# Layer norm tails of a two-block network: the normalization moved to ScalarE, the first turn moved between the last products

## The reference, cut to what matters

```python
def layer_norm(x, g, b):
    mu = x.mean(-1, keepdims=True)
    var = jnp.square(x - mu).mean(-1, keepdims=True)
    y = (x - mu) * lax.rsqrt(var + LN_EPS)
    return y * g + b

for l in range(2):
    mix = hybrid_mixer(x, ...)                      # ends in  y @ w_out[l]
    x = layer_norm(ALPHA * x + mix, ln1_g[l], ln1_b[l])
    ffn = conv_glu_ffn(x, ...)                      # ends in  hidden @ w_down[l]
    x = layer_norm(ALPHA * x + ffn, ln2_g[l], ln2_b[l])
```

## Time and profile before

| | |
|---|---|
| Median of 3 runs | 3353.11 us (3350.36 to 3353.71) |
| Profiled execution | 3352.97 us |
| Span in its profile | 3351.2 us |
| Mean granted clock of TensorE | 0.936 of full speed |
| Busy: TensorE, VectorE, ScalarE, GpSimd | 3006.5, 2480.5, 1366.8, 457.8 us |

### The profile page before, as it was taken

One profiled execution on the slowest core, in us unless ns is written; L12 is line 12 of the kernel. 1 busy time (PEld: TensorE's weight loads), 2 busy tenths in 40 slices (PEclk: granted clock), 3 DMA queues, 4 the chain that ended last, 5 costly groups with the idle time before them and its releaser, 6 DMA issues. The chain is left out here.

```text
span 3351.2 us, 40382 instructions
## 1 busy us (share of the span) xinstructions
PE 3006.5 (90%) x13932; PEld 2421.2 (72%) x13932; DVE 2480.5 (74%) x2722; ACT 1366.8 (41%) x1618; POOL 457.8 (14%) x252
## 2 busy tenths in 40 slices
PE   6997899989878999969997999995997979999995
PEld 5776778867666888747775888884774767888884
DVE  3556798564566997575867999996476658999996
ACT  1131111001231111045235777774336326777774
POOL 0110122321101113210000000001423000000001
PEclk8998899989988999979997999997998979999997
DMA  4231565223233663246219999994212339999993
GB/s 156 69 158 63 178 225 176 101 87 100 97 137 96 207 226 116 86 124 156 75 58 333 373 370 373 385 389 153 101 50 84 120 119 366 375 383 385 385 387 141
DMA packets 346507, 667.25 MB, mean 199 GB/s; under 512 B 21936, under 2 KB 138604, under 8 KB 338172
## 3 DMA queue, kind: packets, MB, share of 16 engines
q1 hardware_dynamic: 339612, 642.58, 54.6%
q0 software_dynamic: 6752, 22.81, 2.0%
HBM read 612.20 MB, written 53.13 MB: 199 GB/s over the span
## 5 line engine op out<-in xcount | busy, mean ns | idle before, releaser
L2683 DVE TENSOR_TENSOR expert_w_low<-expert_w_raw,expert_w_high 128x2048 fp32r<-128x2048 f32 x290 | 663.1, 2289 | 65.4 <-ACT expert_w_high L2644 65.3
L2644 ACT CAST expert_w_high<-expert_w_raw 128x2048 fp32r<-128x2048 f32 x290 | 554.9, 1914 | 181.6 <-PE bank L144 178.7
L142 PE MATMUL bank<-expert_w_high,expert_x_high 128*128 128x512 f32 x928 | 379.7, 409 | 5.2 <-DVE expert_w_low L2683 4.3
L142 PE MATMUL bank<-first_XH,first_w_high 128*128 128x512 f32 x912 | 365.9, 401 | 12.3 <-DVE first_w_low L221 12.3
L144 PE MATMUL bank<-expert_w_high,expert_x_low 128*128 128x512 f32 x928 | 365.3, 394 | 0.0
L143 PE MATMUL bank<-expert_w_low,expert_x_high 128*128 128x512 f32 x928 | 364.0, 392 | 0.0
L143 PE MATMUL bank<-first_XL,first_w_high 128*128 128x512 f32 x912 | 358.5, 393 | 0.0
L144 PE MATMUL bank<-first_XH,first_w_low 128*128 128x512 f32 x912 | 358.3, 393 | 0.0
L221 DVE TENSOR_TENSOR first_w_low<-first_w_raw,first_w_high 128x2048 fp32r<-128x2048 f32 (+2 forms) x104 | 305.3, 2935 | 3.6
L219 DVE CAST first_w_high<-first_w_raw 128x2048 fp32r<-128x2048 f32 (+2 forms) x104 | 120.2, 1156 | 185.2 <-PE bank L144 174.3
L2516 POOL DMA_INDIRECT expert_x_rows<-h_rows,slot_token x58 | 66.4, 1144 | 1265.4 <-PE bank L2549 862.8
(11 more groups left out here) (523 smaller groups left out, 6007.6 us busy)
## 6 DMA issues: line engine op xcount, KB each, us to landing
expert_w_raw<-in_moe_w_gate_dram SPq DMA_DIRECT2D x116, 1024.0 KB, 8.3
expert_w_raw<-in_moe_w_up_dram SPq DMA_DIRECT2D x116, 1024.0 KB, 13.4
expert_w_raw<-in_moe_w_down_dram SPq DMA_DIRECT2D x58, 1024.0 KB, 13.7
modulation<-in_moe_w_down_dram SPq DMA_DIRECT2D x58, 1024.0 KB, 13.8
ffn_mod_w<-in_ada_w_dram SPq DMA_DIRECT2D x48, 1024.0 KB, 5.0
first_w_raw<-in_w_up_dram SPq DMA_DIRECT2D x88, 512.0 KB, 6.2
first_w_raw<-in_w_down_dram SPq DMA_DIRECT2D x22, 1024.0 KB, 4.8
first_w_raw<-in_w_in_dram SPq DMA_DIRECT2D x20, 1024.0 KB, 5.0
```

The costliest lines, as they stand in the source:

```text
L142: nc.tensor.matmul(out, rounded(st[0]), rounded(mv[0]), start=start, stop=False)
L2644: nc.scalar.copy(rounded(high[:, part_of(e, n), :]), weights.place(place)).then_inc(w_high, 1)
L2683: nc.vector.tensor_tensor(rounded(low[:, part_of(e, n), :]), weights.place(place), high[:, part_of(e, n), :], ALU.subtract).then_inc(w_spl ...
```

## The change

In all four tails:

- (X - mean) * rstd goes from VectorE to ScalarE, as Identity(X * rstd + offset) with rstd and offset as one value for each token. VectorE computes the offset, -mean * rstd, by a new instruction on 128x1 after the reciprocal (`deviation`). The weight row (`gain`) stays on VectorE.
- VectorE's order is now stats_of(0), deviation(0), stats_of(1), gain(0), deviation(1), stats_of(2), gain(1), deviation(2), stats_of(3), gain(2), deviation(3), low parts of tile 0, gain(3), low parts of tiles 1 to 3.
- ScalarE's order is, for each tile, Sqrt and Identity; the high parts of tile 0 come after Identity of tile 1, those of tiles 1 to 3 at the end.
- TensorE's order in the last two slots is now a0, a1, b0, a2, b1, a3, turn of tile 0, b2, b3, turns of tiles 1 to 3.
- The waits on split weights (and on the hidden activations' low parts in ffn) stand ahead of every product tile, in all slots.

The diff for mix_out follows. In `ffn_phase` the same edits are made to `turn`, `deviation`, `gain` and to the orders on VectorE and ScalarE, and `last_tiles(DOWN_SLOTS, tile, turn)` takes the place of the loop over the list.

```diff
-def last_tiles(slots):
+def last_tiles(slots, tile, turn):
     a, b = slots - 2, slots - 1
-    return [(a, 0), (a, 1), (b, 0), (a, 2), (b, 1), (a, 3), (b, 2), (b, 3)]
+    for s, t in ((a, 0), (a, 1), (b, 0), (a, 2), (b, 1), (a, 3)):
+        tile(s, t)
+    turn(0)
+    tile(b, 2)
+    tile(b, 3)
+    for t in range(1, TT):
+        turn(t)
...
-def row_products(nc, pe, ps, weights, acts, product_done):
+def row_products(nc, pe, ps, weights, acts, product_done, turn):
     slots = len(weights.loads)
     def tile(s, t):
+        pe.wait_ge(weights.split, s + 1)
         for c in range(2):
...
     for s in range(slots - 2):
-        pe.wait_ge(weights.split, s + 1)
         for t in range(TT):
             last = tile(s, t)
         last.then_inc(weights.used, 1)
-    for s, t in last_tiles(slots):
-        pe.wait_ge(weights.split, s + 1)
-        tile(s, t)
+    last_tiles(slots, tile, turn)
...
         @block.tensor
         def _(pe):
-            row_products(nc, pe, ps, weights, acts, product_done)
-            for t in range(TT):
+            def turn(t):
                 pe.wait_ge(shifted, t + 1)
                 for j in range(2):
                     for i in range(4):
                         k = 4 * j + i
                         last = nc.tensor.transpose(ps[2 * t + j][:, i * P:(i + 1) * P], X[:, t, k * P:(k + 1) * P], ident)
                     last.then_inc(turned, 1)
+            row_products(nc, pe, ps, weights, acts, product_done, turn)
...
-            def norm(t):
+            def deviation(t):
                 dve.wait_ge(std_done, t + 1)
                 chain.link(nc.vector.reciprocal(rstd[:, t:t + 1], std[:, t:t + 1]))
-                nc.vector.tensor_scalar(X[:, t, :], X[:, t, :], mv[:, t, 0:1], rstd[:, t:t + 1], ALU.subtract, ALU.mult
-                                        ).then_inc(normed, 1)
+                nc.vector.scalar_tensor_tensor(offset[:, t:t + 1], mv[:, t, 0:1], -1.0, rstd[:, t:t + 1], ALU.mult, ALU.mult
+                                               ).then_inc(offset_done, 1)
+
+            def gain(t):
                 dve.wait_ge(normed, t + 1)
                 dve.wait_ge(rows_loaded, 32)
                 nc.vector.tensor_tensor(X[:, t, :], X[:, t, :], g_row[:, :], ALU.mult).then_inc(scaled, 1)
...
             for t in range(TT):
                 stats_of(t)
                 if t >= 1:
-                    norm(t - 1)
-            norm(TT - 1)
-            for t in range(TT):
+                    gain(t - 1)
+                deviation(t)
+            split.low_parts(dve, 0)
+            gain(TT - 1)
+            for t in range(1, TT):
                 split.low_parts(dve, t)
...
             for t in range(TT):
                 act.wait_ge(var_done, t + 1)
                 nc.scalar.activation(std[:, t:t + 1], mv[:, t, 1:2], ACT.Sqrt, bias=G["eps_ln"][:, :]).then_inc(std_done, 1)
-            split.high_parts(act)
+                act.wait_ge(offset_done, t + 1)
+                nc.scalar.activation(X[:, t, :], X[:, t, :], ACT.Identity, scale=rstd[:, t:t + 1], bias=offset[:, t:t + 1]
+                                     ).then_inc(normed, 1)
+                if t == 1:
+                    split.high_part(act, 0)
+            for t in range(1, TT):
+                split.high_part(act, t)
```

More of the change, by code:

```diff
@@ L1039, in output_norm_phase @@
         rstd = ph.sb("rstd", [P, TT])
+        offset = ph.sb("offset", [P, TT])
+        offset_done = ph.sem("offset_done")
         rows_loaded = ph.sem("rows_loaded")
@@ L1283, in tile @@
                 toks = slice(t * P, (t + 1) * P)
+                pe.wait_ge(weights.split, FT + s + 1)
+                pe.wait_ge(acts_low, s + 1)
                 for c in range(2):
@@ L1291, in tile, with turn @@
                 return last
+            def turn(t):
+                pe.wait_ge(shifted, t + 1)
+                for j in range(2):
+                    for i in range(4):
+                        k = 4 * j + i
+                        last = nc.tensor.transpose(ps[2 * t + j][:, i * P:(i + 1) * P], X[:, t, k * P:(k + 1) * P], ident)
+                    last.then_inc(turned, 1)
             for s in range(DOWN_SLOTS - 2):
-                pe.wait_ge(weights.split, FT + s + 1)
-                pe.wait_ge(acts_low, s + 1)
                 if s == 0:
@@ L1302, in _ @@
                 last.then_inc(weights.used, 1)
[L1303 to L1313, removed]
+            last_tiles(DOWN_SLOTS, tile, turn)
         @block.scalar
```

## The result

| | before | after |
|---|---|---|
| Median | 3353.71 us, 5 runs (3350.36 to 3355.18) | 3370.53 us, 5 runs (3368.92 to 3372.34) |
| Ratio, 95% interval | | 1.0052 (1.0037 to 1.0067) |
| Span of the profile | 3351.2 us | 3368.7 us |
| Mean granted clock | 0.936 | 0.936 |

The change makes the kernel slower by 16.8 us. The forecast was 3377.4, that is 24.3 more than the 3353.1 it started from, with a range of 3359 to 3384.

What follows compares the result with a forecast made beforehand. TensorE was busy 90% of the span, with time lost where it idles, as in the four layer norm tails. Held product 4 x 1.46, turn 15.7 and clock 2.8 gave 24.3 us on 3353.1: 3377.4, range 3359 to 3384.

Steps and rivals of the forecast that it cites:

- The forecast mechanism: In the four tails: early turn costs 15.7 us, held small product 4 x 1.46 us, granted clock 2.8 us.
- Wait before the first turn: TensorE idles 2.9 to 3.3 us per tail for tile 0; with the turn, tile 2's products come 15.7 us later overall.
- The granted clock in two tails of four: Behind the new wait and turn the clock falls, costing 1.4 us in each of two tails: 2.8 us.
- The small product is held to GpSimd's end: On VectorE, tiles 2 and 3: the 128x1 product waits for GpSimd's addition, over 2 us instead of 0.16.
- VectorE's chain: From the start on tile 2 to the next phase: 23.23 us if held against 21.77 today, 1.46 more per tail.
- Identity on ScalarE: ScalarE's normalization of one tile in the tails: at most 1.56 us, 1.25 taken.
- "not held" rival: VectorE's small product does not wait for GpSimd: 6.1 us more plus 0 to 2.8 for clock, 3359 to 3362; chance 0.18.
- the stretches between unchanged: The phases between the four tails keep their length; only the tails grow, each by about 5.4 us.
- Faster: VectorE's shorter chain wins 4 x 2.41 = 9.6 us, 3343; needs product not held and first turn's tile ready; chance 0.03.

Runs made afterwards that it cites:

- e4: Kernel before with only the change's TensorE order (first turn between the last products) and its waits at every product tile: 3377.34 us, ratio 1.0079.
- e2: Changed kernel with -mean * rstd made by tensor_scalar (one tensor input, rstd as per-partition scalar): 3357.03 us, ratio 1.0015.
- e7: Changed kernel, first turn behind last product, high parts of tile 0 behind all Identities, reciprocal and two-input small product ahead of previous tile's weight row: 3343.45 us.
- e9: Changed kernel, first turn behind last product, one-tensor small product, high parts behind all Identities, weight row of tile 3 ahead of all low parts: 3338.26 us.
- e10: Changed kernel, one-tensor small product, first turn one product tile later (behind b2), high parts of tile 0 behind Identity of tile 2: 3340.6 us, ratio 0.9959.
- e5: Changed kernel with first turn behind the last product, one-tensor small product, high parts of tile 0 behind all four Identities: 3344.89 us, ratio 0.9973.
- e6: Changed kernel with first turn behind the last product and high parts of tile 0 behind all four Identities, small product keeping two inputs: 3361.27 us.

## Why the prediction was right, and where it was off

**The forecast mechanism held.** The held product and the early turn are both there, and in the sizes of the sum.

- *Wait before the first turn.* Forecast 3.28, 2.87, 2.91 and 2.87 us in the order of the tails, measured 3.08, 2.60, 2.71 and 2.60. Most of the difference is how it is counted: the trace counts from the listed end of the last product (319.54 + 0.39), the forecast from 0.226 us behind its start, which gives 3.24 in the first tail. With the turn, VectorE's start on tile 2 was forecast 4.24 us late in the first tail and is 4.22 late. Over the four tails 15.7 + 2.8 (clock) = 18.5 was forecast, 18.62 is measured.
- *The granted clock in two tails of four.* Right in number: it fell in the two ffn tails. Their start on tile 2 is 5.29 us late against 2.87 + 0.96 = 3.83 without the clock, so 1.46 us for it where 1.4 was taken; the second mix_out tail is 3.82 late against 3.87. Which two was not said, so the number is luck in part. Why the clock fell behind 2.60 us of idle time and not behind 3.08 was not predicted and stays open; in e4 it fell behind 4.13 in one mix_out tail and not behind 3.75 in the other.
- *The small product is held to GpSimd's end.* Right: 2.32 and 2.33 us, and e2 and e7 show that for this product it needs both the second SBUF tensor and the addition beside it. The page "SBUF — State Buffer" of the Trainium skill, section "Who interferes with whom", states this rule; the trace agrees with it for a product of 128 values, 2.32 against 0.16 us. It does not agree at L3607: that product has two SBUF inputs as well and began inside a GpSimd instruction that reads SBUF, and it took 0.33 us, to 2570.01, while the next GpSimd instruction starts at 2570.9. The prediction set it aside because that GpSimd instruction has one tensor input. The page makes no such difference, no run here changes GpSimd's instruction, and whether that is the reason is not shown.
- *VectorE's chain.* Forecast +1.46 a tail, measured +1.11, +1.10, +1.12 and +0.73, together 4.06 where 5.84 stood. A held round is 3.54 us (328.56 to 332.10), not 3.70: the 0.16 us of the product lies inside the hold, and the next instruction starts ahead of the listed end. The last tail before had a stall of its own.
- *Identity on ScalarE.* 1.25 taken, 1.24 measured for all 16.

The tails thus give 22.7 us where 24.3 was forecast.

The measured 3370.53 lies just under the 3371 to 3384 that the prediction gave for its forecast alone. It is inside the stated range because that range reaches down to the "not held" rival, which is not what happened.

**The step that failed** is "the stretches between unchanged". The prediction followed the granted clock into the new wait and no further. The phases between the tails spend 4.2 us less at the low clock, in both profiles of the changed kernel, and the 2.1 us by which they are shorter are half of that. The other 3 us between the tails' 22.7 and the difference of the spans lie at the two ends of the span, where two profiles of one kernel differ by up to 6. That explanation is not complete. By their ratios all ten timings with the normalization on ScalarE lie 2 to 5 us under before plus their tails, and e4, which leaves it on VectorE, lies 2 over. No stretch was found that does this in every profile, and it stays open whether it is more than scatter.

**The rivals.** "Not held" is refuted as the description of this change and confirmed as a price, by e9 and by e2, whose tails are 8.4 us longer than before where the rival had 6.1 and 0 to 2.8 for the clock. "Faster" needed, as the prediction has it, a product not held and a first turn that finds its tile ready; e10 has both, and is faster. The rival's 3343 for such a kernel was reached only after two waits that the sum did not have: ScalarE's high parts ahead of Sqrt, and the low parts ahead of the weight row of tile 3. In the change as made the early turn hid both, since it made the high parts ready in time.

## What to carry to other kernels

An instruction put into an in-order queue costs what stands behind it, so place it by when its input is ready: the same turn cost 4 to 5 us a tail ahead of the product tile b2 (e2) and nothing behind it (e10). Before a small VectorE operation with two SBUF tensors is added beside GpSimd, see whether its place is just behind a GpSimd start; put it ahead of what releases GpSimd, or give a small one a single tensor and a scalar for each partition. And when a stall is removed, read the next queue: twice here (e5, e6) 1.6 us of idle time taken away came back as a wait of 1.78 on an instruction with something more urgent behind it.

## What the runs showed of the hardware that was not expected

- The length of the hold has nothing to do with the held instruction: 0.63 us for one that came 1.73 us into an addition, 2.32 for one that came 0.03 us into it, each ending with GpSimd. A `tensor_scalar` of the same size took 0.21 us at the same place.
- The granted clock went to 1.2 GHz behind an idle time of 2.60 us and a turn in the ffn tails, and stayed at 2.4 GHz behind 3.08 and 2.71 us and a turn in the mix_out tails. In e4 it fell behind 4.13 us in the first mix_out tail and stayed behind 3.75 in the second. So the length of the idle time alone does not tell.
- Two executions of one kernel, with spans of 3368.7 and 3362.7 us, were within 0.4 us of each other up to 1474 us, and 6 us apart over the last 1890 us, with the clock at 0.93 and 0.94.
